# HGRN levels of a head in one burst of TensorE products, with halves kept in buffers of their own

## The reference, cut to what matters

```python
def hgrn2_mixer(h, S0, w_in, lb, g_norm, w_out):
    q, fz, i, g = jnp.split(h @ w_in, ...)
    f = lb + (1.0 - lb) * jax.nn.sigmoid(fz)
    k = (1.0 - lb) * jax.nn.sigmoid(-fz)
    q = jax.nn.silu(q)
    # per head, chunked:  A[t, s] = sum_k q[t, k] exp(b[t, k] - b[s, k]) k[s, k]  for s <= t, b = cumsum(log f)
    # o = (q exp(b)) S + A v ;  S = exp(b_last) S + (k exp(b_last - b))^T v
    return rms_norm(o * jax.nn.sigmoid(g), g_norm) @ w_out, S
```

## Time and profile before

| | |
|---|---|
| median of 3 runs | 3158.94 us (3158.48 to 3159.76) |
| the profiled execution | 3158.79 us |
| its span, first to last instruction | 3157.2 us |
| TensorE busy | 3052.8 us |
| VectorE busy | 1917.8 us |
| ScalarE busy | 1172.0 us |
| granted TensorE clock, mean | 0.990 of full speed |
| memory traffic | 269.00 MB, mean 85 GB/s |

### The profile page before, as it was taken

One profiled execution on the slowest core, in us unless ns is written; L12 is line 12 of the kernel. 1 busy time (PEld: TensorE's weight loads), 2 busy tenths in 40 slices (PEclk: granted clock), 3 DMA queues, 4 the chain that ended last, 5 costly groups with the idle time before them and its releaser, 6 DMA issues.

```text
span 3157.2 us, 76452 instructions
## 1 busy us (share of the span) xinstructions
PE 3052.8 (97%) x31972; PEld 2858.8 (91%) x31972; DVE 1917.8 (61%) x3409; ACT 1172.0 (37%) x1971; POOL 131.4 (4%) x247
## 2 busy tenths in 40 slices
PE   8999999999999999998999998999999999999998
PEld 7998999999888999998897777999999998899998
DVE  6777654456676554555547887654555777664454
ACT  4333322223555322224536665322223333422222
POOL 0000000001332000000000000000000000000000
PEclk9999999999999999999999999999999999999999
DMA  3222222223443222222120000222222222222222
GB/s 131 102 95 70 95 87 90 84 101 99 137 129 114 88 86 94 85 97 82 61 75 12 25 26 25 87 87 93 87 95 85 89 88 99 79 84 97 80 94 74
DMA packets 104596, 269.00 MB, mean 85 GB/s; under 512 B 12802, under 2 KB 45954, under 8 KB 104146
## 3 DMA queue, kind: packets, MB, share of 16 engines
q1 hardware_dynamic: 91346, 228.54, 21.8%
q0 software_dynamic: 13056, 37.64, 3.5%
HBM read 247.61 MB, written 18.52 MB: 84 GB/s over the span
## 4 chain that ended last, share of the span: by engine, by line
PE 86%; DVE 7%; ACT 3%; DVEq 2%; issue 1%; DMA 0%; ACTq 0%; SPq 0%
PE ps L671 24%; PE ps L680 14%; PE ps L682 9%; PE ps L683 9%; PE ps L684 9%; PE ps L681 7%; PE ps L1171 3%; PE ps L1149 2%; PE ps L764 1%; PE ps L1181 1%; PE ps L997 1%; PE ps L831 1%; PE ps L1269 1%; PE ps L858 0%; PE ps L768 0%
## 5 line engine op out<-in xcount | busy, mean ns | idle before, releaser
L671 PE MATMUL ps<-arena_r 128*128 128x272 f32 x6768 | 929.8, 295 | 42.3 <-DVE arena_r L2196 19.1
L671 PEld LDWEIGHTS ps<-arena_r 128*128 128x128 f32 x6768 | 875.9, 191 | 79.5 <-issue 52.0
L1597 ACT ACTIVATE arena_r<-ring 128x1024 fp32r<-128x1024 f32 (+1 forms) x240 | 275.1, 1146 | 835.0 <-PE ps L684 820.9
L680 PE MATMUL ps<-hb_r,arena_r 128*128 128x480 f32 x1408 | 537.3, 382 | 3.4 <-DVE arena_r L2228 3.0
L682 PE MATMUL ps<-hb_r,arena_r 128*128 128x304 f32 x1408 | 427.4, 304 | 0.0
L684 PE MATMUL ps<-hb_r,arena_r 128*128 128x304 f32 x1408 | 425.9, 302 | 0.0
L683 PE MATMUL ps<-hb_r,arena_r 128*128 128x304 f32 x1408 | 425.6, 302 | 0.0
L681 PE MATMUL ps<-hb_r,arena_r 128*128 128x240 f32 x1408 | 384.0, 273 | 0.0
L2228 DVE TENSOR_TENSOR arena_r<-ring,arena_r 128x1024 fp32r<-128x1024 f32 (+1 forms) x240 | 318.4, 1327 | 49.4 <-ACT arena_r L1597 49.4
L2262 DVE TENSOR_TENSOR arena<-ps,rstd 128x544 f32<-128x544 f32 x176 | 127.5, 724 | 333.8 <-PE ps L684 333.5
L682 PEld LDWEIGHTS ps<-hb_r,arena_r 128*128 128x128 f32 x1408 | 264.6, 188 | 42.1
(11 more groups left out here) (447 smaller groups left out, 4407.6 us busy)
## 6 DMA issues: line engine op xcount, KB each, us to landing
ring<-in_w_up SPq DMA_DIRECT2D x176, 512.0 KB, 3.4
ring<-in_w_mix SPq DMA_DIRECT2D x112, 512.0 KB, 3.5
ring<-in_w_down SPq DMA_DIRECT2D x64, 704.0 KB, 4.1
arena<-in_hg_s POOLq DMA_DIRECT2D x16, 512.0 KB, 3.7
out_hg_so<-arena POOLq DMA_DIRECT2D x16, 512.0 KB, 2.9
ring<-in_w_hgout SPq DMA_DIRECT2D x16, 512.0 KB, 3.5
arena<-in_cache_k SPq DMA_DIRECT2D x128, 64.0 KB, 1.9
arena<-in_cache_v POOLq DMA_DIRECT2D x128, 64.0 KB, 2.2
```

The lines of the kernel that those rows point to most:

```text
L671: mm = pe.matmul(PS[:, 2 * a + hf, 0:HALF], part[:, ws], rhs[:, o:o + HALF], start=start and n == 0, stop=stop and n == 2)
L680: pe.matmul(both(a), wide, parts[:, :, c, 0:TA], start=start, stop=False, skip_group_check=True)
L1597: act.activation(wh[n % 2][:, 0:width], ring[:, k * SLOT:k * SLOT + width], ACT.Copy)\
```

## The change

The eight levels of a head are multiplied in one burst instead of four. Six further buffers (`hg_u1`, `hg_u[2]` to `hg_u[7]`, one of them, `hg_k0`, for level 0) hold the operands of each level: since level n multiplies the keys of first blocks with the queries of second blocks, one buffer `hg_u[n]` holds both halves. VectorE updates one set of queries and keys in place, and before each update ScalarE has to have copied that half; VectorE's updates and ScalarE's copies signal each other for every half (`lvl`, 16 a head; `kept`, 15 a head). The key turn follows the burst at once. The blocks of the next head are split 21, burst and key turn, 2, states, 5, outputs and the turn of the next head's values, 4 (in the seventh head 2, so that two blocks are left for the last). The next head's first block waits for the emptied value turn (`vt_ev`), whose PSUM bank it overwrites; before the loop the first head's values are turned and emptied behind all four sigmoids. PSUM banks: levels 0 and 1 in bank 5, 2 to 5 in bank 4, 6 and 7 in bank 6, keys in bank 7. ScalarE now places levels 6 and 7 into the scores from PSUM (three copies), VectorE selects 0 and 1 (first signal of `at`) and then 2 to 5 (second). `hg_rest(h + 1, 1)` moves before `inputs`; `hg_rest(h + 1, 4)` before the samples' states, `evict(h + 1, 3)` before `add_head`. In attention one block of the three moves from before the value turn to behind the second turn of probabilities. The number of products and their sizes are the same.

```diff
@@ -322,8 +323,19 @@
 hg_qx, hg_os = ar.take(NB * (NS_TOK + TB)), ar.take(P)
 assert ar.at <= ff_end
-hg_side = (0, 0, 0, 1, 1, 0, 0, 1)
-hg_bank = (4, 5, 6, 7, 4, 5, 6, 7)
+ar = Arena(H, 4 * NT)
+hg_u = [None, hg_u1] + [ar.take(w) for w in (NT, NP_TOK, NP_TOK, NP_TOK)]
+ar = Arena(arena_t, ARENA)
+ar.take(nm_sq_end)
+hg_u += [ar.take(NP_TOK) for _ in range(2)]
+hg_bank = (5, 5, 4, 4, 4, 4, 6, 6)
+hg_col = (0, P, 0, P, 2 * P, 3 * P, 0, P)
+HG_LVL, HG_KEPT = 2 * LEVELS, 2 * LEVELS - 1
+def hg_half(buffer, n, which):
+    size, blk = NT if n <= 2 else NP_TOK, 1 << (n - 1)
+    return buffer[:, 0:size].rearrange("p (m a b) -> p m a b", a=2, b=blk)[:, :, which, :]
 ar = Arena(arena_t, ARENA)
...
@@ -747,6 +759,8 @@
                 if c == 0:
                     if not (head0 and k == 2):
                         pe.wait_ge(S(L + before[k]), h + 1)
+                    if k == 0 and not head0:
+                        pe.wait_ge(S(L + "vt_ev"), h)
...
+        def level_products(n):
+            bank, at = hg_bank[n], hg_col[n]
+            keys, queries = (hg_k0, hg_q) if n == 0 else (hg_u[n], hg_u[n])
+            w = TILE if n < SMALL else 1 << (n - 1)
+            step, off = (w, 0) if n < SMALL else (2 * w, w)
+            for c in range(NCH):
+                for t in range(c * P, (c + 1) * P, step):
+                    mm = pe.matmul(PS[t - c * P:t - c * P + w, bank, at + c * w:at + (c + 1) * w], keys[:, t:t + w],
+                                   queries[:, t + off:t + off + w], start=True, stop=True)
+            if n <= 2:
+                mm = pe.matmul(PS[0:NS_TOK, 5, 2 * P + n * NS_TOK:2 * P + (n + 1) * NS_TOK], keys[:, NP_TOK:NT],
+                               queries[:, NP_TOK:NT], start=True, stop=True)
             return mm
...
-            ahead(3)
-            if more:
-                pe.wait_ge(S(L + "dr_v"), h + 1 + 1)
-                pe.wait_ge(S(L + "state"), h + 1)
-                value_turn(h, 6)
-                ahead(4)
-            else:
-                pe.wait_ge(S(L + "state"), h + 1)
+            ahead(21)
+            if not more:
+                project(h, 4 * KC - 2, 4 * KC)
+                for m, c in ((0, 0), (0, 1), (0, 2), (1, 0), (1, 1), (0, 3), (1, 2), (1, 3)):
+                    out_block(m, c)
+            pe.wait_ge(S(L + "kept"), (h + 1) * HG_KEPT)
+            for n in range(LEVELS):
+                mm = level_products(n)
+            mm.then_inc(S(L + "lvl_mm"), 1)
+            pe.wait_ge(S(L + "lvl"), h * HG_LVL + HG_LVL - 1)
+            for c in range(NCH):
+                pe.transpose(PS[:, 7, c * P:(c + 1) * P], hg_ks[:, c * P:(c + 1) * P], const("ident"))
+            pe.transpose(PS[:, 6, 3 * P:4 * P], hg_ks[:, NP_TOK:NP_TOK + P], const("ident")).then_inc(S(L + "kt_mm"), 1)
+            ahead(2)
+            if not more:
+                out_block(0, 4)
+                out_block(1, 4)
             pe.wait_ge(S(L + "vt_ev"), h + 1)
...
+            pe.wait_ge(S(L + "kt_ev"), 3 * h + 1)
+            pe.wait_ge(S(L + "at"), 2 * h + 1)
...
+            pe.wait_ge(S(L + "kt_ev"), 3 * h + 2)
...
-            ahead(2)
+            ahead(5)
             if not more:
-                out_block(0, 4)
-                out_block(1, 4)
                 out_block(0, 5)
+                out_block(1, 5)
             pe.wait_ge(S(L + "s"), h + 1)
+            pe.wait_ge(S(L + "at"), 2 * h + 2)
+            pe.wait_ge(S(L + "kt_ev"), 3 * h + 3)
...
                 if c:
-                    pe.matmul(PS[:, 4, cs], hg_s[:, (c - 1) * P:c * P], hg_qp[1][:, cs], start=False, stop=True)
-            if not more:
-                out_block(1, 5)
+                    pe.matmul(PS[:, 4, cs], hg_s[:, (c - 1) * P:c * P], hg_qp[:, cs], start=False, stop=True)
             pe.wait_ge(S(L + "smp_ev"), h + 1)
             pe.matmul(PS[:, 5, 0:NS_TOK], hg_os, const("stack"), start=True, stop=True).then_inc(S(L + "o_mm"), 1)
-            if hand:
+            if more:
                 pe.wait_ge(S(L + "dr_v"), h + 2 + 1)
                 value_turn(h + 1, 0)
-                ahead(4)
-            else:
-                ahead(6)
+            ahead(2 if hand else 4)
             if not more:
                 out_block(0, 6)
...
                 pe.wait_ge(S(L + "wl"), 4 * HEADS * (j + 1) + KC * j + m + 1)
+                if m == 0:
+                    pe.wait_ge(S(L + "vt_ev"), HEADS * (j + 1))
...
@@ -893,6 +885,8 @@
         norm(norm_name(layer, "m"), 2)
         project(j * HEADS, KC, 4 * KC, head0=True)
         pe.wait_ge(S("norm_rms"), nth(norm_name(layer, "m")) + 1)
+        pe.wait_ge(S(L + "dr_v"), j * HEADS + 2)
+        value_turn(j * HEADS, 0)
         with pe.Fori(j * HEADS, (j + 1) * HEADS - 2) as h:
...
-            ahead(3, 0)
+            ahead(2, 0)
             pe.wait_ge(S("at_ev_v"), h + 1)
             for c in range(NCH):
                 pe.transpose(PS[:, 0, c * P:(c + 1) * P], at_v[:, c * P:(c + 1) * P], ident)
             pe.transpose(PS[:, 1, 0:P], at_v[:, NT - P:NT], ident).then_inc(S("at_vt_mm"), 1)
             turn(1)
-            ahead(1, 0)
+            ahead(2, 0)
             weigh(0)
...
+        def first_keys(h):
+            act.wait_ge(S(L + "lvl"), h * HG_LVL + 1)
+            act.activation(hg_k0, hg_sgn, ACT.Copy, scale=scratch[:, 1:2]).then_inc(S(L + "kept"), 1)
+            act.activation(hg_half(hg_u[1], 1, 0), hg_half(hg_sgn, 1, 0), ACT.Copy, scale=scratch[:, 1:2]).then_inc(S(L + "kept"), 1)
+        def kept_queries(h, n):
+            act.wait_ge(S(L + "lvl"), h * HG_LVL + (2 if n == 1 else 2 * n - 1))
+            act.activation(hg_half(hg_u[n], n, 1), hg_half(hg_qp, n, 1), ACT.Copy).then_inc(S(L + "kept"), 1)
+        def kept_keys(h, n):
+            act.wait_ge(S(L + "lvl"), h * HG_LVL + 2 * n)
+            act.activation(hg_half(hg_u[n], n, 0), hg_half(hg_ks, n, 0), ACT.Copy).then_inc(S(L + "kept"), 1)
+        def kept(h, n):
+            kept_queries(h, n)
+            kept_keys(h, n)
         def mix(h, more, hand=False):
-            if more:
-                value_turned(h, 6)
-                kept_halves(h, 2)
+            first_keys(h)
+            if more:
                 done(base, h + 1, 0)
                 hg_split(layer, h + 1, 2)
-                kept_halves(h, 4)
+                kept_queries(h, 1)
+                for n in range(2, LEVELS):
+                    kept(h, n)
                 raw(h + 1, 0, split=False)
                 done(base, h + 1, 1)
                 hg_split(layer, h + 1, 3)
-                kept_halves(h, 6)
+            else:
+                kept_queries(h, 1)
+                high(L, V_HG + j, o3, hh, 0)
+                kept(h, 2)
+                high(L, V_HG + j, o3, hh, 1)
+                kept(h, 3)
+                raw(h, 3)
+                for n in range(4, LEVELS):
+                    kept(h, n)
+                    high(L, V_HG + j, o3, hh, n - 2)
+                high(L, V_HG + j, o3, hh, KC - 2)
+            act.wait_ge(S(L + "kt_mm"), h + 1)
+            act.activation(hg_kt, PS[:, 7, :], ACT.Copy).then_inc(S(L + "kt_ev"), 1)
+            act.activation(hg_kts[0:2 * NS_TOK, :], PS[0:2 * NS_TOK, 6, 3 * P:4 * P], ACT.Copy)
+            for n in range(SMALL, LEVELS):
+                w = 1 << (n - 1)
+                for t in range(0, P, 2 * w):
+                    cp = act.activation(hg_at[t:t + w, :].rearrange("p (c t) -> p c t", c=NCH)[:, :, t + w:t + 2 * w],
+                                        PS[t:t + w, 6, hg_col[n]:hg_col[n] + NCH * w].rearrange("p (c t) -> p c t", c=NCH), ACT.Copy)
+            cp.then_inc(S(L + "kt_ev"), 1)
+            if more:
                 raw(h + 1, 1, split=False)
+            act.wait_ge(S(L + "at"), 2 * h + 2)
+            for ts in hg_blocks:
+                cp = act.activation(hg_at[ts, :].rearrange("p (c t) -> p c t", c=NCH)[:, :, ts],
+                                    hg_atc[ts, :].rearrange("p (c t) -> p c t", c=NCH), ACT.Copy)
+            cp.then_inc(S(L + "kt_ev"), 1)
+            if more:
+                raw(h + 1, 2)
...
-            if hand:
+            if more:
                 value_turned(h + 1, 0)
-            elif more:
-                raw(h + 1, 2)
...
         for k in range(4):
             raw(j * HEADS, k, True)
+        value_turned(j * HEADS, 0)
...
+        def next_level(h, n, dprev, doff):
+            size, blk = NT if n <= 2 else NP_TOK, 1 << (n - 1)
+            m = size // (2 * blk)
+            dv = dprev[:, 0:size // blk].rearrange("p (m a) -> p m a", a=2)
+            dn = hg_d[:, doff:doff + m]
+            dve.drain()
+            dve.tensor_tensor(dn, dv[:, :, 0], dv[:, :, 1], ALU.mult)
+            def queries():
+                dve.wait_ge(S(L + "kept"), h * HG_KEPT + (3 if n == 1 else 2 * n))
+                dve.tensor_tensor(hg_half(hg_qp, n, 1), hg_half(hg_qp, n, 1), dv[:, :, 0:1].to_broadcast([P, m, blk]), ALU.mult)\
+                   .then_inc(S(L + "lvl"), 1)
+            def keys():
```

(54 more changed lines are left out.)

168 lines of the change are left out of this document (13 added, 155 removed).

## The result

The changed kernel takes **3179.0 us** (median of four runs, 3178.2 to 3184.7) against 3158.7 for the kernel before (four runs, 3155.8 to 3159.8): ratio 1.0070, 95% interval 1.0058 to 1.0082. It is slower by 20.3 us, where 8 were forecast; the sign was right, the size was 12 us short, and the time lies 1 us outside the range. The profiled execution took 3178.6 us, its span 3177.0, 19.8 more than the span before.

A forecast was written before the change was run, and what follows sets the result against it. TensorE, busy 97% of the span, was taken to bound the kernel. Steady heads -5.5, first heads +6.2, last heads +4.8, clock +2.4 and attention zero summed to +7.9: 3167 us, range 3152 to 3178.

The forecast's parts named there:

- Steady heads: Twelve HGRN heads: 32.93 us each without new waits, 33.86 with TensorE waiting 0.95; 0.46 gained each, -5.5 us.
- First heads: First head of each layer: TensorE waits 2.0 us for the emptied value turn; +3.1 us each, +6.2.
- The number of products is the same.: TensorE's work in a head: the product count stays, so fewer bursts and a covered key turn save 1.39 us.
- Clock: Four long waits, at layer starts and in last heads: some lower the granted clock, 1.6 us each; +2.4 us taken.
- Last heads: Last head of each layer: output blocks wait 9.2 us for VectorE's remainders, the sixth 1.8 more; +2.4 each, +4.8.
- Attention: One block moved behind the second probability turn: new idle of 0.7 us swallows a later wait; zero, between -1 and +3.
- The first: Steady heads: kept halves end by 19.5 us, so the burst is not waited for; -7.7 us, 3151; chance 0.17.
- The second: Waits between engines remove the 0.09 us overlap, 0.8 us a head; 11 us more, 3178; chance 0.15.
- The third: Layer ends cheaper: clock stays up, TensorE's waits in the last head are half; +2.2 us, 3161; chance 0.20.

The follow-up runs named there:

- order: Changed kernel, but ScalarE copies level 1's queries before it splits the next weights: ratio 1.0026 to the kernel before, median 3166.0 us.
- split: Changed kernel with the burst cut in two and three of the 21 blocks before it moved between the halves: ratio 1.0033, median 3167.2 us.
- Double: Changed kernel with every product of the burst issued twice: 3246.9 us (one run).
- no split: The kernel with all three edits, but with one burst instead of two halves: ratio 1.0019 to the kernel before, median 3163.7 us.
- cut1: The kernel with all three edits, but one block in place of three between the halves of the burst: 3160.8 us (one run).
- the kernel with all three edits: Changed kernel: burst cut in two, first head's value turn moved earlier, level 1's queries copied before ScalarE's split, old attention: ratio 0.9991, median 3155.7 us.

## Why the prediction was right and wrong

**Steady heads: right.** Forecast 33.86 us, -0.46 each; measured 33.91, -0.40. From the value turn to the burst it is 20.47 us (20.42 laid out), behind it 13.44 (13.44). Waits make the head 0.98 longer than 32.93, where 0.95 was laid out; the idle times recorded, 0.36 and 0.32, sum to less, for they count from the end of the last product and not from where the next would have started. The sum of the three bursts that go is 0.93, not 0.95, which changes nothing. The run "order" shows the reason too: ScalarE's place for one copy.

**First heads: right.** Forecast +3.1 each. In "split", where no stop is in them, they are 3.21 and 3.24 longer than before, and the wait behind the turn is 1.89 us, forecast 2.0.

**The step that failed: "The number of products is the same."** It priced 222 short products in a piece by rows in which 32 or 64 stand in a piece, in a loop that repeats, and put the supply of instructions at nothing. In code that runs for the first time the burst stops for 1.7 to 2.15 us, in four of the six such bursts: 7.4 us, and low clock behind two of them; the first heads and the seventh of layer 0 are 3.6 us longer than the stops explain (0.3, 1.75 and 1.5; behind the last two stops the clock is low for 3.4 us each). That is 11 of the 12 us between forecast and result; the cut took 10.3 off. "Double", "no split" and "cut1" show that the stops go by a run of short products in unseen code, and the places of the stops and the packets in front of them that it is the loading of instructions, 256 at a time. Open is why a packet is not asked for earlier.

**Clock: mis-sized.** Forecast +2.4. Measured by lengths at either clock, the last heads lose 3.35 us to it in layer 0 (36 products take 6.4 us where 4.6 were due, and 5.64 us stand from the last waiting block to the stack product against 4.13 in layer 3) and 1.5 in layer 3 (6.1 for the 36). With 3.55 behind the stops, and 1.8 back in the rest of the program, that is +6.6. The 1.8 is a balance: two low stretches of the kernel before, behind the output parts (332.7 and 2722.0 us), are gone, for 1.5 each, and others grow. The forecast took one row with a known price once and a half; there were six stretches.

**Last heads: right in size.** Forecast +2.4 each. Measured +7.3 and +3.6; without the stop of 1.68 and what the clock took, +2.3 and +2.1. The waits were 2.35, 0.97, 4.64 and none (8.0 in sum) against 9.2 laid out for the first four blocks, and 1.61 against 1.8 for the sixth. Part of that 1.2 is clock again: the block in front of the wait of 4.64 took 1.73 us, where the one before it took 0.99.

**Attention: right,** zero.

Summed: -5.1 (twelve heads at their own pace) + 7.4 (stops) + 6.45 (first heads) + 4.4 (last heads) + 6.6 (clock and the rest) = 19.75, against 19.8 of span.

**Rivals.** The first (burst not waited for) fell for the change as it stands, and "order" comes most of the way to what it asked for, with one copy 0.66 us earlier (10.20 instead of 10.86 us behind the value turn) and not with less work: the burst starts at 19.84, where the rival had 19.5. The second gave nearly the measured time, 3178, from a cause that isn't there: steady heads would be 34.7 us. The Trainium skill (VectorE: DVE Perf Modes, "The DRAIN you can't avoid") says that the next operation does not start before the pipe is empty, and in the same section that one which isn't held starts earlier. The changed kernel's trace shows the second: VectorE's keys have a wait for ScalarE's copy in front of them, and still start 0.33 us after queries of 0.42.

```profile
98.27 0.42 DVE L2396 TENSOR_TENSOR arena<-arena 128x256 f32<-128x256 f32 x1
98.60 0.42 DVE L2402 TENSOR_TENSOR arena<-arena 128x256 f32<-128x256 f32 x1
```

A time that fits is no proof of a cause; the head's length told them apart. The third fell with the clock and with last heads as long as forecast.

## What to carry to other kernels

Price a burst of very short products twice: once in a loop that repeats, once in code that runs for the first time. There it can run out of instructions: count 128 products with their weight loads as a piece, and hold the time that they take (1.6 us here) against the 3.5 to 4.0 us in which pieces came. A few long blocks in the middle of the burst fill the difference: three of them took the stops from 6.7 us to 0.65 and left the steady heads as they were (0.04 us less each). When a copy for a later engine is added, put it ahead of work that waits for something else: one line moved gave 0.64 us a head. And weigh a part by its own length between two fixed instructions, over several runs: what the change did not touch differed here by 8 us from profile to profile.

## What the runs showed that was not expected

- Stops without a releaser inside a burst of 222 products (level 7's have 64 columns, the others 32) that lasts 2.75 us, only where the code is new: 1.7 to 2.15 us each; with 444 products 14 stops of up to 2.6 us, 128 products apart, each 2.2 to 2.9 us behind the start of a 16 KB packet of instructions.
- Low clock of 3.4 to 10.2 us at a time, behind stops of under 2 us too; in the kernel with all three edits such stretches still make 27.3 us of the two layers, against 6.8 before. In front of a wait for VectorE they cost nothing.
- The same untouched code took between 2575.8 and 2583.7 us.
